# A chunked two-direction scan: one direction moved to the other quarters of the array, part of an element product given to GpSimd

## The chip, the cores and the metric

One core of a Trainium2 chip runs the whole kernel in one launch. The metric is the device time of that launch in microseconds, the median of several runs. The work of this case is all in one stage of the kernel, a recurrent scan of some 306 us out of about 2309 us.

## The reference, cut to what matters

The reference is a two-block model on 1024 tokens of width 1024, with 256 context tokens ahead. The change touches only the linear recurrence of the first block, run for 8 heads of 64 channels in both directions over 256 + 1024 tokens:

```
def wkv_scan(state0, r, decay, kk, b, v, k, reverse):
    def step(S, inp):
        r_t, w_t, kk_t, b_t, v_t, k_t = inp
        sa = jnp.einsum("bhvk,bhk->bhv", S, kk_t)
        S = (S * w_t[:, :, None, :] - sa[..., None] * b_t[:, :, None, :]
             + v_t[..., None] * k_t[:, :, None, :])
        return S, jnp.einsum("bhvk,bhk->bhv", S, r_t)
    ...
    S, ys = lax.scan(step, state0, xs, reverse=reverse)
```

All of it is float32.

## The kernel before, in words

**Stages.** `projections` (names `b_`) makes r, k, v, the decays and the keys, and stores four operands per direction and head pair to HBM (`ops`). `scan` (names `c_`) runs the recurrence; `mix_up` and the rest follow it and need its output `y`. The stages come one after the other.

**The scan.** The tokens are cut into chunks of 64; 4 context chunks and 16 sequence chunks make 20 steps (`STEPS`), `s` from 0. Direction `x` = 0 takes the chunks forwards, `x` = 1 backwards; both do step `s` at the same time. The 8 heads are 4 pairs `q`, and in a pair head `h` lies on partitions 0 to 63 or 64 to 127 (`ROWS[h]`). TensorE works with tiles of its array: a 64x64 matmul reads one half of the partitions and writes one half, so it occupies one of four quarters of the array. In what follows a quarter is named by the half it reads and the half it writes. Each float32 matmul appears in the trace as two records.

**TensorE's order in a step** is written out by hand (L1303 to L1325); every part is called for direction 0 and then for direction 1 by `both_dirs`:
- L1252 `chain_g_values`: both directions read the upper half and write lower and upper;
- L1214 `token_major`: 128x128 transposes of the next step's operands; L1261 `chain_g_state`: both directions read and write the same half (lower to lower, upper to upper);
- L1221 `triangles`: 64x128 matmuls of the next step; L1270 `chain_z`: both directions read both halves and write the lower one;
- L1277 `chain_s`, L1190 `blocks` (four of the twenty steps), L1232 `level_y` (32x32 tiles, next step), L1285 and L1288 `chain_y` (from step 4 on), L1242 `last_u` (next step).

A part's last matmul of a direction raises that direction's semaphore. ScalarE copies the results out of PSUM in the same order (`c_bk`, `c_gg`, `c_vz`, `c_raw`, `c_yd`, `c_ud`). VectorE masks the triangles (L1419, `c_lm`, two instructions per direction), makes the new state (L1423, L1425), and adds `y` in the later steps (L1406).

**The inverses.** Every four chunks (a batch `T`, five in all) need the inverse of triangular blocks. VectorE makes them in four parts (`blocks(T, part)`), one part behind each step's state; two batches go ahead of the loop in part (all of batch 0, parts 0 and 1 of batch 1), and step 0 has parts 2 and 3 of batch 1. Steps 1 to 12 have the parts 0 to 3 of batches 2, 3 and 4, one each. A product is a `dot`: an element product into `c_mul` (L1441, 512 to 2048 elements a partition) and a sum over the inner axis (L1442). The next step's L1419 stands behind the part on VectorE's queue. GpSimd only turns the finished inverse (L1527, `c_ti`) and, after the last one, splits weights for the next stage (L1530 to L1537).

**The DMA queue.** All DMAs here are issued in order by SyncE (SP): the stores of `ops` in `projections` (L220), 16 small stores of raw blocks (L312), a last operand store and a store of `mixd` (L238), then waits for all of them; the scan starts with the load of the first blocks (L1105, `c_nb`).

## Time and profile before

| | us |
|---|---|
| median of 3 runs | 2309.03 (2307.44 to 2312.41) |
| the profiled execution's own time | 2308.51 |
| its span | 2306.7 |
| scan, from its first load at 487.78 to its last VectorE instruction at 793.85 | 306.1 |

The span is the profiled part of that execution; the 1.8 us around it belong to the launch. PE is TensorE's matmuls, PEld its weight loads, DVE VectorE, ACT ScalarE, POOL GpSimd, SPq the DMAs that SyncE issues. A row of the timeline gives start, duration, engine, line, operation, output and inputs, shapes and how many instructions are merged; in square brackets stands the idle time ahead and what ended it.

### The profile page before, as it was taken

The numbers are of one execution on the slowest core, as the hardware profiler recorded it, in microseconds if no ns is written. First come the engines' busy times: TensorE is split into PE (matmuls) and PEld (weight loads), VectorE is DVE, ScalarE is ACT, GpSimd is POOL, SyncE is SP. The second block draws the span as 40 slices with busy tenths as digits, with TensorE's granted clock in tenths as the row PEclk, the third lists the DMA queues.
The fourth block names the chain that finished last, engine by engine and source line by source line (L and its number), as shares of the span: only waits on it lengthen the run. The fifth ranks groups of instructions, "written<-read, shape, count | busy, mean of one in ns | idle before, by whom it ended". The sixth has DMA issues, their size and how long they took to land. (4 is left out here: it accounts for less than half of the span.)

```text
span 2306.7 us, 36893 instructions
## 1 busy us (share of the span) xinstructions
PE 2108.3 (91%) x15096; PEld 1633.8 (71%) x15096; DVE 1543.7 (67%) x1999; ACT 872.2 (38%) x1411; POOL 782.9 (34%) x461
## 2 busy tenths in 40 slices
PE   7779999946999999899999989999899999999898
PEld 1656776745888777688887767887677777776666
DVE  5887767778887356888888892246636665545644
ACT  3434444412443355533333332354524343333320
POOL 0424344400003042777777753434222101111111
PEclk9889999976999999999999999999999999999999
DMA  7463343476765432122122255433212111102512
GB/s 285 176 214 112 108 141 112 133 210 177 201 198 140 134 119 86 52 83 79 70 80 83 83 187 205 152 114 109 84 56 83 56 32 61 65 19 68 197 55 82
DMA packets 180838, 271.07 MB, mean 118 GB/s; under 512 B 73784, under 2 KB 121528, under 8 KB 176320
## 3 DMA queue, kind: packets, MB, share of 16 engines
q1 hardware_dynamic: 176064, 251.94, 33.3%
q10 hardware_dynamic: 4608, 16.78, 2.0%
q8 instruction: 121, 1.98, 0.4%
q14 instruction: 45, 0.37, 0.1%
HBM read 200.48 MB, written 68.19 MB: 116 GB/s over the span
## 5 line engine op out<-in xcount | busy, mean ns | idle before, releaser
L105 PE MATMUL b_ps<-h_hi,b_wpool 128*128 128x512 f32 (+1 forms) x976 | 300.2, 385 | 20.3 <-issue 7.5
L2932 PE MATMUL g_ps<-g_h_hi,w 128*128 128x512 f32 x784 | 258.2, 401 | 5.0 <-ACT g_q L3125 5.0
L3245 POOL TENSOR_TENSOR w<-raw_down,w 128x1024 fp32r<-128x1024 f32 x38 | 94.3, 2482 | 460.0 <-ACT w L3103 460.0
L105 PEld LDWEIGHTS b_ps<-h_hi,b_wpool 128*128 128x128 f32 x976 | 182.4, 192 | 69.4 <-issue 19.8
L2201 DVE SCALAR_TENSOR_TENSOR e_vars<-grid,vec,e_vars 128x1024 f32<-128x1024 f32 x168 | 216.0, 1286 | 7.5 <-ACT e_vars L1948 4.2
L105 PE MATMUL b_ps<-h_lo,b_wpool 128*128 128x512 f32 (+1 forms) x488 | 184.5, 378 | 0.0
L2932 PEld LDWEIGHTS g_ps<-g_h_hi,w 128*128 128x128 f32 x784 | 147.6, 188 | 39.2 <-ACT g_q L3125 5.7
L2932 PE MATMUL g_ps<-g_h_lo,w 128*128 128x512 f32 x392 | 154.6, 394 | 0.0
L2613 POOL TENSOR_TENSOR g_down_lo<-raw_down,g_down_hi 128x1408 fp32r<-128x1408 f32 x26 | 86.6, 3335 | 141.6 <-ACT g_down_hi L2513 141.6
L2452 PE MATMUL g_pb<-g_z_hi,g_down_hi 128*128 128x512 f32 x286 | 114.6, 401 | 14.8 <-DVE g_down_lo L2690 9.8
L713 POOL TENSOR_TENSOR b_wpool<-raw_in,b_wpool 128x1024 fp32r<-128x1024 f32 x26 | 66.7, 2564 | 169.2 <-ACT b_wpool L511 169.2
L2452 PE MATMUL g_pb<-g_z_hi,g_down_lo 128*128 128x512 f32 x286 | 112.9, 395 | 0.0
L2452 PE MATMUL g_pb<-g_z_lo,g_down_hi 128*128 128x512 f32 x286 | 112.3, 393 | 0.0
L1928 ACT ACTIVATE e_main_hi<-e_raw_up 128x512 fp32r<-128x512 f32 x68 | 41.9, 622 | 172.1 <-DMA e_raw_up<-w_ffn 169.8
L105 PEld LDWEIGHTS b_ps<-h_lo,b_wpool 128*128 128x128 f32 x488 | 94.0, 193 | 16.8 <-issue 1.5
L2042 POOL TENSOR_TENSOR e_main_lo<-e_raw_up,e_main_hi 128x512 fp32r<-128x512 f32 x68 | 92.5, 1364 | 15.6 <-ACT e_main_hi L1928 15.6
L1527 POOL COPY c_ti<-c_ui 128x1024 f32<-128x1024 f32 x5 | 9.8, 1968 | 245.3 <-DVEq L1490 245.3
L3393 DVE COPY g_pt<-g_pb 128x512 f32<-128x512 f32 (+2 forms) x144 | 74.2, 552 | 18.9 <-PE g_pb L2991 17.6
L3025 PE MATMUL g_ps<-g_h_hi,w 128*128 128x512 f32 x224 | 77.9, 418 | 9.0 <-DVE g_sq L3401 3.3
L2932 PEld LDWEIGHTS g_ps<-g_h_lo,w 128*128 128x128 f32 x392 | 73.9, 189 | 16.2 <-issue 0.7
L3423 DVE SCALAR_TENSOR_TENSOR raw_down<-g_ps,g_gs 128x128 f32<-128x128 f32 x32 | 9.3, 292 | 108.1 <-PE g_ps L3007 108.1
L2250 DVE TENSOR_TENSOR e_z<-e_act_g,combine 128x512 f32<-128x512 f32 x42 | 63.6, 1553 | 22.4 <-ACT e_act_g L1961 22.3
(508 smaller groups left out, 5437.6 us busy)
## 6 DMA issues: line engine op xcount, KB each, us to landing
e_raw_up<-w_ffn SPq DMA_DIRECT2D x22, 1024.0 KB, 4.9
raw_down<-w_down SPq DMA_DIRECT2D x32, 704.0 KB, 4.1
c_op<-ops SPq DMA_DIRECT2D x40, 512.0 KB, 4.9
raw_down<-w SPq DMA_DIRECT2D x38, 512.0 KB, 3.7
b_xin<-ada_rows ACTq DMA_DIRECT2D x32, 512.0 KB, 5.1
ops<-b_xin SPq DMA_DIRECT2D x16, 1024.0 KB, 4.2
raw_in<-w SPq DMA_DIRECT2D x26, 512.0 KB, 4.2
zs<-e_z SPq DMA_DIRECT2D x21, 512.0 KB, 2.6
```

Source lines behind the costliest of these rows:

```text
L105: last = nc.tensor.matmul(out, w[:, k, :], x[:, k, cols], start=(k == 0 and n == 0), stop=(k == nk - 1 and n == 2))
L713: TT(weights(s)[1], raw, weights(s)[0].bitcast(F32), ALU.subtract).then_inc(sem("lo"), 1)
L1928: A(w_hi[slot], a_of[slot] if i < PLAIN else source[slot], ACT.Copy).then_inc(sem(f"w_hi{slot}"), 1)
L2042: TT(w_lo[slot], a_of[slot] if i < PLAIN else source[slot], w_hi[slot].bitcast(F32), ALU.subtract).then_inc(sem(f"w_lo{slot}"), 1)
L2201: STT(out=acc, in0=view, scalar=wt, in1=acc, op0=ALU.mult, op1=ALU.add).then_inc(sem("conv"), 1)
L2250: a = TT(z[:, cols(g)], act_g[:, cols(g)], val_of(g, i), ALU.mult)
L2452: mm = nc.tensor.matmul(bank_of(g, j), w[s][:, k], y[:, f], start=(f == 0 and i == 0), stop=(f == NFF - 1 and i == 2))
L2613: nc.gpsimd.tensor_tensor(w_lo[w_slot(n)], raw[:, n % 2], w_hi[w_slot(n)].bitcast(F32), ALU.subtract).then_inc(sem(f"w_lo{n % 2}"), 1)
L2932: mm = nc.tensor.matmul(out_bank, ww[w % 2][:, k], xx[g][:, k], start=(k == 0 and a == 0), stop=(k == KD - 1 and a == 2))
L3025: mm = nc.tensor.matmul(ps[1][:], ww[w % 2][:, k], xx[g][:, k], start=(a == 0 and b == 0), stop=(a == 1 + LAST and b == 2))
L3245: nc.gpsimd.tensor_tensor(w_lo[w % 2], raw[:, w % 2], w_hi[w % 2].bitcast(F32), ALU.subtract).then_inc(sem("lo"), 1)
L3393: nc.vector.tensor_copy(pt[:, h, at // P:to // P].rearrange("p b c -> p (b c)"), turned[u % 2][:, 0:to - at]).then_inc(sem("unturned"), 1)
```

## The change

The backward direction's operands are stored with the heads' halves exchanged and in another order (stores and loads L220, L1089, a table of decays exchanged by way of HBM), so that its `chain_g_values`, `chain_g_state`, `chain_z` and the first half of `chain_y` use the two quarters of the array that the forward direction doesn't use. These parts (and `blocks`) are no longer called once per direction: the matmuls of the two directions alternate, both directions' waits stand ahead of the part, and both semaphores are raised at its end. In the loop `triangles` of direction 0 now stands ahead of `chain_z` and that of direction 1 behind it.

In the two `dot`s with 2048 elements of each inverse batch (`c_nb,c_ui` in part 2, `c_ui,c_wi` in part 3) VectorE multiplies the first 10 of 16 rows (or 5 of 8), 1280 elements; GpSimd multiplies the other 768 into the same buffer. VectorE raises `part_due` ahead of its own product, and waits for `part_made` ahead of the sum.

```diff
-                sp.dma_start(d["ops"][x, :, s0:s0 + n // C, m],
-                             ops[:, j % 2, 0:n // C].rearrange("p s a c -> p s (a c)")).then_inc(sem(f"ops_stored{j % 2}"), 16)
+                for to, rows in (((slice(0, P), slice(0, P)),) if x == 0 else ((slice(0, HEAD), slice(HEAD, P)), (slice(HEAD, P), slice(0, HEAD)))):
+                    sp.dma_start(d["ops"][x, to, s0:s0 + n // C, m],
+                                 ops[rows, j % 2, 0:n // C].rearrange("p s a c -> p s (a c)")).then_inc(sem(f"ops_stored{j % 2}"), 16)
...
+            sp.dma_start(d["pends"], t["pend"][:, 1, NCTX:SLOTS]).then_inc(sem("pend"), 16)
...
+                            rows, of = slice(HEAD * h, HEAD * (h + 1)), slice(HEAD * (h ^ x), HEAD * ((h ^ x) + 1))
...
-    R, KK, B, K = range(4)
+    R, KK = (0, 3), (1, 2)
+    W_R, W_KK = (0, 1), (1, 0)
+    PAIR_RK, PAIR_BK = (slice(0, 2), slice(2, 4)), (slice(2 * C, 4 * C), slice(0, 2 * C))
...
-        OF_B, OF_K = ROWS
+        OF_B, OF_K = ROWS, ROWS[::-1]
+        state = lambda x, h: ROWS[h ^ x]
+        level = lambda x: slice(OF_B[x].start + HB * x, OF_B[x].start + HB * (x + 1))
...
+            for h in HEADS:
+                sp.dma_start(t["pend"][ROWS[h], 1, NCTX:SLOTS], d["pends"][ROWS[1 - h]]).then_inc(sem("pend"), 16)
...
-            def chain_g_state(x, s):
-                wait("p_gv", x, s + 1)
-                wait("sc", x, s + 1)
-                for q in range(PAIRS):
-                    for rows in ROWS:
-                        mm = nc.tensor.matmul(half(bank[x][2])[rows, q], op[x][s % 3][rows, KK, q], sc[x][s % 2][rows, q],
-                                              start=False, stop=(q == PAIRS - 1))
-                mm.then_inc(S("p_g", x), 1)
...
+            def chain_g_state(s):
+                for x in DIRS:
+                    wait("p_gv", x, s + 1)
+                    wait("sc", x, s + 1)
                 for q in range(PAIRS):
                     for h, rows in enumerate(ROWS):
-                        mm = nc.tensor.matmul(z_out(x, h)[OF_B, q], ud[x][s // BATCH % 2][rows, place(x, s), q], gg[x][rows, q], start=True, stop=True)
-                mm.then_inc(S("p_z", x), 1)
+                        mm = [nc.tensor.matmul(half(bank[x][2])[rows, q], op[x][s % 3][state(x, h), KK[x], q], sc[x][s % 2][state(x, h), q],
+                                               start=False, stop=(q == PAIRS - 1)) for x in DIRS]
+                for x in DIRS:
+                    mm[x].then_inc(S("p_g", x), 1)
...
+            def chain_z(s):
+                for x in DIRS:
+                    wait("u", x, s + 1)
+                    wait("gg", x, s + 1)
+                for q in range(PAIRS):
+                    for h, rows in enumerate(ROWS):
+                        mm = [nc.tensor.matmul(z_out(x, h)[OF_B[x], q], ud[x][s // BATCH % 2][rows, place(x, s), q], gg[x][rows, q],
+                                               start=True, stop=True) for x in DIRS]
+                for x in DIRS:
+                    mm[x].then_inc(S("p_z", x), 1)
...
+                        mm = nc.tensor.matmul(half(bank[x][2])[state(x, h), q], bk[x][s % 2][:, q, h ^ x], vz[x][s % 3][:, h, q], start=True, stop=True)
...
+            def chain_y(s):
+                for x in DIRS:
+                    wait("s1", x, s + 1)
+                out = [half(bank[x][2], 1) for x in DIRS]
                 for q in range(PAIRS):
                     for h, rows in enumerate(ROWS):
-                        mm = nc.tensor.matmul(out[rows, q], vz[x][s % 3][:, h, q], lm[x][s % 2][:, h, q, 0], start=False, stop=(q == PAIRS - 1))
-                mm.then_inc(S("p_y", x), 1)
+                        for x in DIRS:
+                            nc.tensor.matmul(out[x][rows, q], sc[x][s % 2][state(x, h), q], op[x][s % 3][state(x, h), R[x], q],
+                                             start=(q == 0), stop=False)
+                for x in DIRS:
+                    for q in range(PAIRS):
+                        for h, rows in enumerate(ROWS):
+                            mm = nc.tensor.matmul(out[x][rows, q], vz[x][s % 3][:, h, q], lm[x][s % 2][:, h, q, W_R[x]], start=False, stop=(q == PAIRS - 1))
+                    mm.then_inc(S("p_y", x), 1)
...
-                both_dirs(chain_g_values, s)
+                chain_g_values(s)
                 if more:
                     both_dirs(token_major, u)
-                both_dirs(chain_g_state, s)
+                chain_g_state(s)
                 if more:
-                    both_dirs(triangles, u)
-                both_dirs(chain_z, s)
+                    triangles(0, u)
+                chain_z(s)
+                if more:
+                    triangles(1, u)
                 both_dirs(chain_s, s)
                 if s in pres:
-                    both_dirs(blocks, pres[s])
+                    blocks(pres[s])
                 if more:
                     both_dirs(level_y, u)
                 if has_y(s):
-                    both_dirs(chain_y, s)
+                    chain_y(s)
...
+                if s == 0 and x == 1:
+                    dve.wait_ge(sem("pend"), 32)
...
+            def shared_dot(out, left, right, negate, nth):
+
+                rows, js, cols = *left.shape[1:], right.shape[2]
+                mine = slice(0, rows * 5 // 8)
+                prod = mul[:, 0:rows * cols * js].rearrange("p (i k j) -> p i k j", i=rows, k=cols)
+                dve.sem_inc(sem("part_due"), 1)
+                done(TT(prod[:, mine], bc(left[:, mine], 2, cols), bc(right.rearrange("p j k -> p k j"), 1, rows * 5 // 8), ALU.mult))
+                dve.wait_ge(sem("part_made"), nth)
...
-                    dot(w[:, :, low], n12, u22[:, :, low], False)
+                    shared_dot(w[:, :, low], n12, u22[:, :, low], False, 2 * T + 1)
...
-                    dot(u12[:, top], u11[:, top], w, True)
+                    shared_dot(u12[:, top], u11[:, top], w, True, 2 * T + 2)
...
+            def part_dot(left, right, nth):
+                rows, js, cols = *left.shape[1:], right.shape[2]
+                mine = slice(rows * 5 // 8, rows)
+                prod = mul[:, 0:rows * cols * js].rearrange("p (i k j) -> p i k j", i=rows, k=cols)
+                pool.wait_ge(sem("part_due"), nth)
+                nc.gpsimd.tensor_tensor(prod[:, mine], bc(left[:, mine], 2, cols), bc(right.rearrange("p j k -> p k j"), 1, rows - rows * 5 // 8),
+                                        ALU.mult).then_inc(sem("part_made"), 1)
...
+                part_dot(n12, u22[:, :, m // 2:m], 2 * T + 1)
+                part_dot(u11[:, 0:m // 2], w, 2 * T + 2)
```

TensorE's order for one step without `blocks` and `chain_y`, first as before (from L1252, `chain_g_values`, to L1242, `last_u`):

```order
L1252 MATMUL c_ps<-c_vz,c_lm 64x64 x16
L1214 MATMUL c_ps<-con,c_op 128x128 x8
L1261 MATMUL c_ps<-c_sc,c_op 64x64 x16
L1221 MATMUL c_ps<-c_op 128x128 x16
L1270 MATMUL c_ps<-c_gg,c_ud 64x64 x16
L1277 MATMUL c_ps<-c_vz,c_bk 64x64 x16
L1232 MATMUL c_ps<-c_td,c_lm 32x32 x16
L1242 MATMUL c_ps<-c_ud,c_yd 32x32 x16
```

And the same step with the change (L1266 is now `chain_g_values`, L1234 `triangles`, L1288 `chain_z`, L1297 `chain_s`):

```order
L1266 MATMUL c_ps<-c_vz,c_lm 64x64 x16
L1227 MATMUL c_ps<-con,c_op 128x128 x8
L1277 MATMUL c_ps<-c_sc,c_op 64x64 x16
L1234 MATMUL c_ps<-c_op 128x128 x8
L1288 MATMUL c_ps<-c_gg,c_ud 64x64 x16
L1234 MATMUL c_ps<-c_op 128x128 x8
L1297 MATMUL c_ps<-c_vz,c_bk 64x64 x16
L1245 MATMUL c_ps<-c_td,c_lm 32x32 x16
L1255 MATMUL c_ps<-c_ud,c_yd 32x32 x16
```

The number of matmuls is the same; the sixteen `triangles` now stand in two groups of eight on either side of `chain_z`.

GpSimd's order in the scan, before (L1527 turns the five inverses, the casts and subtractions are the next stage's weights):

```order
L1527 COPY c_ti<-c_ui 128x1024 x5
L1530 CAST c_hc<-c_hc 128x1024
L1532 TENSOR_TENSOR c_hc<-c_hc 128x1024
L1530 CAST c_hc<-c_hc 128x1024
L1532 TENSOR_TENSOR c_hc<-c_hc 128x1024
```

And with the change (L1560 is the part of the element product, L1569 the turn):

```order
L1560 TENSOR_TENSOR c_mul<-c_nb,c_ui 128x768
L1560 TENSOR_TENSOR c_mul<-c_ui,c_wi 128x768
L1569 COPY c_ti<-c_ui 128x1024
L1560 TENSOR_TENSOR c_mul<-c_nb,c_ui 128x768
L1560 TENSOR_TENSOR c_mul<-c_ui,c_wi 128x768
L1569 COPY c_ti<-c_ui 128x1024
```

Two products of 768 elements stand ahead of each of the five turns, ten in all.

## Rows read from the trace of the kernel before

**Rows 1.** Windows: length, busy of PE, PEld, DVE, ACT, POOL (count), PEclk, DMA share, GB/s.
```profile
487.78:523.80 36.02, 16.73 (x296) 15.39 (x296) 33.71 (x43) 5.32 (x10) 0.02 (x1) 0.64 0.84 234
...
564.57:722.00 157.43, 143.93 (x3582) 130.37 (x3584) 134.86 (x203) 64.72 (x189) 5.89 (x4) 0.92 0.65 181
...
745.23:779.01 33.78, 32.95 (x892) 30.00 (x890) 15.56 (x30) 13.58 (x42) 1.88 (x2) 1.00 0.36 105
```

**Rows 2.** VectorE's waits, 564.57 to 722.00 (total us, times, longest).
```profile
DVE c_lm L1419 <- PE c_ps L1221: 13.6, 6, 5.2
DVE c_s L1423 <- PE c_ps L1277: 2.7, 6, 0.8
DVE c_y L1406 <- PE c_ps L1288: 2.4, 2, 1.3
```

**Rows 3.** Timeline of TensorE, one late step.
```profile
774.63 1.15 PE L1252 MATMUL c_ps<-c_vz,c_lm 64*64 64x64 f32 x32
...
776.73 1.15 PE L1261 MATMUL c_ps<-c_sc,c_op 64*64 64x64 f32 x32
777.80 2.06 PE L1221 MATMUL c_ps<-c_op 64*128 64x128 f32 x32
...
781.22 1.23 PE L1277 MATMUL c_ps<-c_vz,c_bk 128*64 128x64 f32 x32 [0.28 <-ACT c_vz L1332]
782.37 0.60 PE L1232 MATMUL c_ps<-c_td,c_lm 32*32 32x32 f32 x32
782.90 0.68 PE L1285 MATMUL c_ps<-c_op,c_sc 64*64 64x64 f32 x16
```

**Rows 4.** Timeline of TensorE in the last step, where two parts meet.
```profile
786.82 0.27 PE L1261 MATMUL c_ps<-c_sc,c_op 64*64 64x64 f32 x1
786.87 0.22 PE L1252 MATMUL c_ps<-c_vz,c_lm 64*64 64x64 f32 x2
```

**Rows 5.** Timeline of VectorE, part 2 of an inverse and what follows.
```profile
645.56 3.79 DVE L1441 TENSOR_TENSOR c_mul<-c_nb,c_ui 128x2048 f32<-128x2048 f32 x1
649.39 2.29 DVE L1442 TENSOR_REDUCE c_wi<-c_mul 128x128 f32<-128x2048 f32 x1
651.82 1.92 DVE L1441 TENSOR_TENSOR c_mul<-c_ui,c_wi 128x1024 f32<-128x1024 f32 x1
...
655.03 2.48 DVE L1419 TENSOR_TENSOR c_lm<-c_ps,con_mixer 128x512 f32<-128x512 f32 x4
657.43 0.41 DVE L1423 TENSOR_TENSOR c_s<-c_sc,c_ps 128x256 f32<-128x256 f32 x1
```

**Rows 6.** Timeline of VectorE and GpSimd where both multiply at once.
```profile
69.07 2.83 DVE L918 TENSOR_TENSOR h_lo<-b_xin,h_hi 128x2560 fp32r<-128x2560 f32 x1
69.11 6.08 POOL L733 TENSOR_TENSOR h_lo<-b_xin,h_hi 128x1536 fp32r<-128x1536 f32 x1 [3.63 <-DVE b_xin L911]
...
735.59 2.35 POOL L1532 TENSOR_TENSOR c_hc<-c_hc 128x1024 fp32r<-128x1024 f32 x1
736.03 2.19 DVE L1425 TENSOR_TENSOR c_sc<-c_s,pend 128x256 f32<-128x256 f32 x1
```

**Rows 7.** Timeline of GpSimd around 722.
```profile
721.98 2.00 POOL L1527 COPY c_ti<-c_ui 128x1024 f32<-128x1024 f32 x1 [54.91 <-DVEq L1490]
723.92 1.04 POOL L1530 CAST c_hc<-c_hc 128x1024 fp32r<-128x1024 f32 x1
```

**Rows 8.** Windows with TensorE's granted clock, columns as in Rows 1.
```profile
562.00:564.00 2.00, 0.00 (x0) 0.00 (x0) 1.97 (x2) 0.00 (x0) 0.00 (x0) 0.50 0.00 0
570.00:572.00 2.00, 2.00 (x21) 1.88 (x18) 1.86 (x11) 0.25 (x1) 0.00 (x0) 0.50 0.74 116
...
604.00:606.00 2.00, 0.68 (x26) 0.43 (x22) 2.00 (x5) 0.28 (x1) 0.00 (x0) 1.00 1.19 368
```

**Rows 9.** DMAs issued by SyncE between the two stages.
```profile
480.87 0.45 SPq L220 DMA_DIRECT2D ops<-b_xin  x1
...
487.78 0.33 SPq L1105 DMA_DIRECT2D c_nb<-pb  x1
```

More of the change, by code:

```diff
@@ L1058, in scan, with tiles @@
                 if (s + 10) % BATCH < 2 and (s + 10) // BATCH < NBATCH}
+        def tiles(buf, m, row, col):
+            n, size = HB // (2 * m), 2 * m * (HB + 1)
+            start = row * HB + col
+            part = buf[:, 0:n * size].rearrange("p (b z) -> p b z", z=size)
+            end = start + m * HB
+            if end > size:
+                return buf[:, start:end].rearrange("p (b i c) -> p b i c", b=1, c=HB)[:, :, :, 0:m]
+            return part[:, :, start:end].rearrange("p b (i c) -> p b i c", c=HB)[:, :, :, 0:m]
         block = st.enter_context(nc.Block())
@@ L1184, in _ @@
         def _(pe):
-            def heads(out, *pairs):
-                for q in range(PAIRS):
-                    for n, (still, moving) in enumerate(pairs):
-                        for rows in ROWS:
-                            last = nc.tensor.matmul(out[rows, q], still[rows, q], moving[rows, q],
-                                                    start=(n == 0), stop=(n == len(pairs) - 1))
-                return last
             def wait(name, x, value):
@@ L1244, in last_u, with chain_g_values @@
                 mm.then_inc(S("p_u", x), 1)
-            def chain_g_values(x, s):
-                wait("lm", x, 2 * s + 2)
-                wait("s1", x, s)
-                wait("yo", x, s - NCTX)
+            def chain_g_values(s):
+                for x in DIRS:
+                    wait("lm", x, 2 * s + 2)
+                    wait("s1", x, s)
+                    wait("yo", x, s - NCTX)
                 for q in range(PAIRS):
                     for h, rows in enumerate(ROWS):
-                        mm = nc.tensor.matmul(half(bank[x][2])[rows, q], lm[x][s % 2][OF_K, h, q, 1], vz[x][s % 3][OF_K, h, q],
-                                              start=(q == 0), stop=False)
-                mm.then_inc(S("p_gv", x), 1)
@@ L1256, in chain_g_state @@
-            def chain_g_state(x, s):
-                wait("p_gv", x, s + 1)
-                wait("sc", x, s + 1)
-                for q in range(PAIRS):
-                    for rows in ROWS:
-                        mm = nc.tensor.matmul(half(bank[x][2])[rows, q], op[x][s % 3][rows, KK, q], sc[x][s % 2][rows, q],
-                                              start=False, stop=(q == PAIRS - 1))
-                mm.then_inc(S("p_g", x), 1)
-            def chain_z(x, s):
-                wait("u", x, s + 1)
-                wait("gg", x, s + 1)
+                        mm = [nc.tensor.matmul(half(bank[x][2])[rows, q], lm[x][s % 2][OF_K[x], h, q, W_KK[x]], vz[x][s % 3][OF_K[x], h, q],
+                                               start=(q == 0), stop=False) for x in DIRS]
@@ L3556, in constants @@
     before = [s < u, s > u]
-    parts["tri"] = np.concatenate([tri(m) for b in before for m in (b | (s == u), b)], 1)
+    parts["tri"] = np.concatenate([tri(m) for x, b in enumerate(before) for m in ((b | (s == u), b), (b, b | (s == u)))[x]], 1)
     first = np.tile(np.arange(C), BANK // C)[None, :]
```

83 lines of the change are left out of this document (39 added, 44 removed).

## The prediction, made before the changed kernel ran

> **What bounds the kernel now.** I read the timeline of the scan first, then windows of it, then VectorE's waits, and last the places where GpSimd works beside VectorE. The scan falls into three stretches, and each has another bound. Ahead of step 0 VectorE makes the first inverse: in the 36.02 us up to its first mask it is busy 33.71, TensorE 16.73 [rows 1]. In the twelve inverse steps (from the mask at 564.57 to that at 722.00, 157.43 us) the two are close: TensorE busy 143.93, VectorE 134.86 [rows 1]. VectorE waits there 13.6 + 2.7 + 2.4 = 18.7 us for TensorE [rows 2], so without any wait it would need 157.4 - 18.7 = 138.7 us. That is the floor which VectorE's queue sets, since the next step's mask stands behind the inverse's part. In the late steps, which have no inverse, TensorE is busy 32.95 of 33.78 us for three steps, 11.26 us each [rows 1]: there it alone sets the end.
>
> **TensorE's quarters.** A part of 32 records in two quarters takes 1.15 us, and the next may start 1.07 us after it (776.73 to 777.80) [rows 3]. Does a third or fourth quarter run beside them? The last step shows it: a record of L1261 (lower half to lower half, direction 0) starts at 786.82 while L1252 (upper half to both halves, direction 1) is still putting in two records at once at 786.87 [rows 4]. So a quarter takes its records when it is free, whatever the others do. The 32x32 part issues 32 records in 0.53 us (782.37 to 782.90) [rows 3], so issue isn't a limit before about 17 ns a record, and I take 0.54 for a part of four quarters. Each of `chain_g_values`, `chain_g_state` and `chain_z` gets shorter by 0.53 us; of `chain_y` the two first halves, 0.61 each (the 0.68 of L1285 less its 0.07 of overlap) [rows 3], become one of 0.55, so 0.67. The wait of 0.28 us for ScalarE ahead of `chain_s` [rows 3] goes too, because direction 1's triangles (half of 2.06) stand there now. Sum for a late step: 3 x 0.53 + 0.67 + 0.28 = 2.54 us, from 11.26 to 8.72.
>
> What is late next: direction 1's triangles come behind `chain_z`, and VectorE masks them (half of 2.48) before it makes any state; then come state, scaling and state, about 0.42 each with gaps of 0.03 to 0.04 [rows 5], and `chain_y` now waits for the states of both directions. That is 0.2 (end of the matmuls) + 1.24 + 1.35 = 2.8 us behind the triangles, of which `chain_s` (1.15) and `level_y` (0.53) cover 1.7. So 1.1 us of wait come back, and 0.1 ahead of `chain_z`, whose two copies on ScalarE are now covered by half the triangles. The step becomes 8.72 + 1.2 = 9.9 us, a gain of 1.3.
>
> The Trainium skill's page "TensorEngine Tiling (Array Packing)", section "Restrictions and Gotchas", says that different row tiles can't use the same PSUM bank at once. By that rule L1261, whose two halves write one bank, would be slower than L1252, whose two tiles are in one row; both take 1.15 us, so the trace doesn't bear it out. Were it so with four quarters, the parts would keep their length, and the time would be that of the third rival below.
>
> **GpSimd's share.** The change supposes that GpSimd multiplies beside VectorE. The rows say that it can't. At 69.07 VectorE begins a product of two SBUF tensors, at 69.11 GpSimd one; VectorE takes its 2.83 us, and GpSimd, with 1536 elements, 6.08: 2.83 of waiting and 3.25 of work [rows 6]. At 736.03 it is the other way round: L1425 takes 2.19 us, because GpSimd's subtraction lasts until 737.94 [rows 6]. The inverse's product L1441 has two inputs in SBUF as well. VectorE raises `part_due` and goes on at once, so it begins first; GpSimd then multiplies its 768 elements while VectorE waits for `part_made`. The two run one behind the other.
>
> What GpSimd needs for 768 elements isn't in the trace. At 3.25 us for 1536 it would be 1.6; but one operand is read with a step, and a copy of 1024 elements that reads with a step takes 2.00 against 1.04 for a plain cast [rows 7], 0.94 ns an element more: 0.7 us more with one such operand at the 2.35 us per 1024 of L1532 (1.8), or 1.9 times the 1.8. So 1.6 to 3.4; I take 1.8 + 0.7 = 2.5, since L1532 and L1527 are the nearest rows. VectorE saves 3/8 of 3.79 = 1.42, and pays 0.1 for raising a semaphore (the gap of 0.14 at 651.68, where one is raised already, against 0.04) [rows 5]. Each of the ten products so costs 2.5 + 0.1 - 1.4 = 1.2 us on VectorE, between 0.3 and 2.1.
>
> The page "GPSIMD Engine Reference", section "Instruction dispatch", of the Trainium skill gives a floor of 2.5 cycles per element for two inputs, at 1.2 GHz. An estimate by that page is 1.6 us for 768, and the total below would be some 9 us less; no run here shows a product with this step on GpSimd.
>
> **The sum, stretch by stretch.** Ahead of the scan SyncE issues one more half store and the decays' store behind the store that takes 0.45 us at 480.87; the first load of the scan waits for all of them [rows 9]: +0.9. The twelve other split stores lie beside TensorE's dense work in the stage before and cost nothing; if a weight load queued behind them were late, 0.4 each. The decays' two loads stand ahead of loads that are not needed until step 4: nothing. The first inverse is all VectorE's: two products, +2.4. Step 0 holds two more, again with TensorE idle behind them: +2.4; ahead of them TensorE's shorter parts bring VectorE's next mask forward by about 1.0, since the mask of direction 1 now waits for `chain_z`: -1.0.
>
> In the twelve inverse steps the shorter parts put TensorE mostly behind VectorE, so the floor counts: 138.7 + 6 x 1.2 = 145.9. It isn't reached. In a part-2 step VectorE needs 655.03 - 645.56 = 9.5 us for the part [rows 5] and 4.0 for masks and states, 13.5 us from mask to mask, 14.7 with the share, and TensorE some 9, so it idles for 5 us. After such idleness the granted clock is 0.50, the lower level of 1.2 GHz, as at 562 to 564, and stays there while TensorE works again (570 to 572: busy all the time, 0.50); at 604 to 606, after less idleness, it is 1.00 [rows 8]. One such drop in each of the three batches makes TensorE late by 1.5 to 2 us, and the parts with `blocks`, where ScalarE's two copies now come one behind the other, by some more: +6. So 152, a gain of 5.4. Late steps: three at 1.3, -3.9; the two ahead of them, where GpSimd's subtractions hold up L1425 as before, 0.9 each, -1.8; the tail, which is a chain of latencies, -0.8.
>
> Total: 0.9 + 2.4 + 2.4 - 1.0 - 5.4 - 3.9 - 1.8 - 0.8 = -7.2. From the profiled execution's 2308.5 (0.5 under the median, which is less than the runs differ by) this gives **2301**. With GpSimd at its bounds (0.3 and 2.1 for each of ten products) it is 2292 and 2310.
>
> **Rivals.**
> *The products do run side by side.* Then GpSimd ends about 2.6 us after the start, and a product costs 1.0 less than before instead of 1.2 more. For: another access pattern on VectorE, which takes 1.85 ns an element, may leave the port free. Against: both places in [rows 6]. The first inverse and step 0 gain 2 x 2.0 instead of losing 4.8; the inverse steps have a floor of 138.7 - 6 = 132.7, and with TensorE's remaining 6 end near 138.7, -18.7. Total 0.9 - 2.0 - 3.0 - 18.7 - 6.5 = -29.3: 2279.
> *TensorE's clock falls in every inverse step (slower).* TensorE's shorter parts leave it idle in all of them, not in three. For: a drop shows at 562. Against: 604 to 606. At 1.2 GHz the way from a mask to the next (waits of 1.3, `level_y`, `chain_y`, `last_u`, `chain_g_values`, transposes, `chain_g_state`, half the triangles: about 6 us at full clock without the 1.3) doubles to 12, and with the mask's 2.48 a step takes 14.4: 12 x 14.4 = 172.8, +15.4. Total 3.3 + 1.4 + 15.4 - 6.5 = +13.6: 2322. It decides once more than half of the twelve steps run at the low clock.
> *The other quarters bring nothing (slower).* The parts keep their length, so only the new waits stay: late steps 0.4 longer, +2; the waits of [rows 2] remain and six products add about 6; ahead +5.7. Total +13.7: 2322. Against it: [rows 4].
>
> **Chances and range.** The forecast 0.55, side by side 0.15, clock 0.18, quarters 0.12. The likeliest case alone spans 2292 to 2311. The range that takes in the first rival's time and most of the slower ones, which reach down towards 2312 where they hold in part, is 2279 to 2320. No change is within 0.2% (4.6 us) of 2309, about what a measurement can tell. Of the forecast's 0.55 some 0.36 lie under 2304, 0.16 between, 0.03 above 2314; with the rivals: faster 0.51, the same 0.19, slower 0.30.
>
> **What would show it.** `chain_g_state` and its like at about 0.75 us long instead of 1.15; late masks 9.9 us apart; L1560 on GpSimd at over 4 us when its wait behind VectorE is counted, and 2.5 from the end of VectorE's product; VectorE idle by 2.5 ahead of each of ten sums; the granted clock low once per batch. I am wrong if GpSimd's product ends with VectorE's, if the four-quarter parts still take over 1.0 us, or if the low clock fills the inverse steps.

## The result, and the profile after

The changed kernel takes 2315.48 us (median of 20 runs, 2304.69 to 2326.76), the kernel before beside it 2306.02 (20 runs, 2301.05 to 2323.1). The ratio is 1.0033, 95% interval 1.0020 to 1.0046: slower by 7.6 us, 4.6 to 10.6. (The two medians stand 9.5 apart, inside that interval; what follows goes by the ratio.) The forecast was 2301 and faster. The profiled execution took 2320.37 us (span 2318.6), 11.9 us of span more than that of before. It is 4.9 us above its kernel's median, so a pair of single traces has more to explain than the timed runs do.

Four places say most of it. First the windows of the changed kernel, columns as in [rows 1] and answering to them:

```profile
491.81:529.41 37.60, 11.50 (x296) 10.09 (x296) 35.07 (x43) 5.54 (x10) 4.37 (x3) 0.59 0.82 225
570.20:722.82 152.62, 126.41 (x3584) 110.92 (x3584) 138.40 (x203) 66.01 (x192) 19.97 (x10) 0.88 0.67 187
746.65:783.30 36.65, 29.88 (x893) 26.30 (x897) 15.13 (x30) 13.89 (x42) 1.93 (x2) 0.95 0.36 107
```

The twelve inverse steps are shorter (152.62 for 157.43 in this pair of traces), and TensorE is busy 126.41 us there for 143.93. But three late steps take 36.65 us where they took 33.78, although TensorE is busy 3.1 us less. That is the surprise: it has less to do and is done later.

TensorE's timeline in the late steps (start, length, line, tiles, count, idle time and what ended it), which answers to [rows 3]:

```profile
739.50 1.04 PE L1307 MATMUL c_ps<-c_op,c_sc 64*64 64x64 f32 x32 [2.32 <-DVE c_s L1451]
740.48 1.97 PE L1312 MATMUL c_ps<-c_lm,c_vz 128*64 128x64 f32 x32
...
756.36 0.69 PE L1277 MATMUL c_ps<-c_sc,c_op 64*64 64x64 f32 x32
756.98 1.16 PE L1234 MATMUL c_ps<-c_op 64*128 64x128 f32 x16
758.07 0.69 PE L1288 MATMUL c_ps<-c_gg,c_ud 64*64 64x64 f32 x32
758.70 0.60 PE L1234 MATMUL c_ps<-c_op 64*128 64x128 f32 x5
761.47 0.94 PE L1234 MATMUL c_ps<-c_op 64*128 64x128 f32 x11 [2.17 <-issue]
```

The four-quarter parts are what they were forecast to be: `chain_g_state` (L1277) is 0.69 us long and the next part starts 0.62 after it, against 1.15 and 1.07 [rows 3]. Two things stand between them now. One is a wait for VectorE of 2.32 us ahead of `chain_y`, followed by a second half at half the speed (1.97 us for the 1.15 that the same part has elsewhere). The other is an idle time of 2.17 us in the middle of a part, after five of its sixteen records, which ends on "issue": no semaphore was waited for.

The same wait from the other engines' side, and the first of the shared products (VectorE and GpSimd in one timeline):

```profile
512.46 2.21 POOL L1560 TENSOR_TENSOR c_mul<-c_nb,c_ui 128x768 f32<-128x768 f32 x1 [42.09 <-DVEq L1467]
512.47 4.44 DVE L1468 TENSOR_TENSOR c_mul<-c_nb,c_ui 128x1280 f32<-128x1280 f32 x1
...
736.40 2.34 POOL L1574 TENSOR_TENSOR c_hc<-c_hc 128x1024 fp32r<-128x1024 f32 x1
...
737.05 1.98 DVE L1453 TENSOR_TENSOR c_sc<-c_s,pend 128x256 f32<-128x256 f32 x1
```

The product runs one behind the other, as forecast, but GpSimd is first: 2.21 us for its share, and VectorE's 4.44 us are these and some 2.2 of its own. At 737.05 VectorE's scaling (0.42 us when alone) stands behind GpSimd's subtraction until 738.74, as at 736.03 in [rows 6]. That hold made TensorE wait in the kernel before too, but only 0.78 us; its step took 12.59 us there, the three behind it 11.26:

```profile
738.61 0.68 PE L1285 MATMUL c_ps<-c_op,c_sc 64*64 64x64 f32 x16 [0.78 <-DVE c_s L1423]
```

The groups of products, of before (first fence) and after: line, tiles, count, busy us, mean ns.

```profile
L1441 DVE TENSOR_TENSOR c_mul<-c_nb,c_ui 128x2048 f32<-128x2048 f32 x5 | 18.9, 3787 | 0.0
L1441 DVE TENSOR_TENSOR c_mul<-c_ui,c_wi 128x2048 f32<-128x2048 f32 x5 | 18.3, 3652 | 0.1
```

```profile
L1468 DVE TENSOR_TENSOR c_mul<-c_nb,c_ui 128x1280 f32<-128x1280 f32 x5 | 22.3, 4456 | 0.1
L1468 DVE TENSOR_TENSOR c_mul<-c_ui,c_wi 128x1280 f32<-128x1280 f32 x5 | 21.4, 4273 | 0.3
L1560 POOL TENSOR_TENSOR c_mul<-c_nb,c_ui 128x768 f32<-128x768 f32 x5 | 11.8, 2368 | 145.1 <-DVEq L1467 145.1
```

Ten products hold VectorE for 43.7 us instead of 37.2, 0.65 more each.

SyncE's issues between the two stages (start, length of issue), answering to [rows 9]:

```profile
463.37 9.81 SPq L221 DMA_DIRECT2D ops<-b_xin  x3
473.23 9.14 SPq L313 DMA_DIRECT2D pb<-h_spare  x16
482.41 1.26 SPq L221 DMA_DIRECT2D ops<-b_xin  x2
483.72 1.94 SPq L316 DMA_DIRECT2D pends<-pend  x1
485.70 2.18 SPq L239 DMA_DIRECT2D mixd<-c_row  x1
491.81 0.32 SPq L1121 DMA_DIRECT2D c_nb<-pb  x1
```

The last operand store's two halves take 1.3 us to issue where the whole took 0.45, the decays' store 1.9, and the issue of `mixd` grew from 0.58 to 2.18. From 463.37 to the scan's first load it is 28.44 us; before, 25.92. The long issues are not the sixteen small stores' doing, for the 0.45 and 0.58 of before stood behind the same sixteen. What stands ahead of them is an operand store. Behind the whole one at 471.31 two issues were long in the kernel before as well, the second and the third of the sixteen:

```profile
472.34 1.24 SPq L312 DMA_DIRECT2D pb<-h_spare  x1
473.63 0.75 SPq L312 DMA_DIRECT2D pb<-h_spare  x1
...
481.37 0.58 SPq L238 DMA_DIRECT2D mixd<-c_row  x1
```

In the changed kernel the decays' store and `mixd` stand in that place behind two halves, and take more.

Last, windows over the late steps, the tail and the next stage's start, of before (first fence) and after, columns as in [rows 1]; the clock is the third figure from the end:

```profile
722.00:779.01 57.01, 53.95 (x1446) 48.69 (x1442) 28.54 (x50) 22.64 (x70) 21.44 (x15) 1.00 0.51 142
779.01:793.90 14.89, 13.73 (x400) 12.29 (x396) 7.37 (x16) 4.65 (x16) 0.00 (x0) 1.00 0.01 3
793.90:804.00 10.10, 8.78 (x31) 5.95 (x32) 3.11 (x3) 2.12 (x2) 0.00 (x0) 1.00 0.78 286
```

```profile
722.82:783.30 60.48, 49.72 (x1438) 43.89 (x1442) 28.15 (x50) 21.90 (x66) 21.49 (x15) 0.92 0.48 133
783.30:800.00 16.70, 12.72 (x400) 11.30 (x400) 7.46 (x16) 4.88 (x16) 0.00 (x0) 0.83 0.01 3
800.00:810.00 10.00, 8.75 (x24) 5.24 (x25) 1.88 (x2) 1.06 (x1) 0.00 (x0) 0.77 0.78 287
```

Before, TensorE worked at 2.4 GHz from 722 to 804 without a break; now it falls to 1.2 GHz for part of each of these stretches.

**What the idle times on "issue" are.** Twelve times in the scan TensorE stands still with its semaphores reached. I counted TensorE's records (matmuls, weight loads, waits) up to the one that ends each, and looked for the last 16 KB instruction fetch (DMA queue 8) before it. Worked out from the trace's records, not a view:

```
from    idle  line   record    of 256  fetch began  resumed after it
552.90  0.83  L1255   5058      194     551.30       +2.43
558.07  0.28  L1288   5314      194     555.91       +2.44
636.89  2.64  L1255   8642      194     637.19       +2.34
651.88  1.13  L1255   9409      193     650.26       +2.74
657.32  0.36  L1288   9666      194     655.23       +2.46
677.70  0.66  L1266  10690      194     675.91       +2.46
700.17  1.32  L1307  11713      193     698.77       +2.72
721.54  1.11  L1234  12738      194     720.14       +2.51
749.57  0.46  L1245  14017      193     747.55       +2.48
753.23  1.48  L1266  14274      194     752.39       +2.32
759.30  2.17  L1234  14530      194     758.97       +2.50
775.47  0.75  L1307  15297      193     773.82       +2.40
```

All twelve (the first expectation below counts eleven) end at the same place modulo 256 records, 193 or 194, and 2.3 to 2.75 us after a 16 KB fetch began: TensorE had come to the end of a block of 256 instructions, and the next was still on its way. They sum to 13.2 us, against 4.3 in five such places before, and 5.9 in a second trace of the kernel before. These idle times are called stalls below.

The Trainium skill's page "Runtime: NRT & Kernel Launch", section "Instruction fetch mechanics", says that instructions are refilled in blocks of 256 (16 KiB) while the block ahead runs, and that crossing a block is mostly hidden. The trace agrees on the block's size; hidden it isn't in these twelve places.

### The profile page after: what moved, and what is told of

It reads as the page before. It is cut to its first block and busy times, and to the rows that moved or that the text cites. A ratio compares the mean times of both kernels' runs of the same rounds, so it can differ in the third digit from the quotient of the medians.

```text
span 2318.6 us, 36973 instructions
## 1 busy us (share of the span) xinstructions
PE 2083.9 (90%) x15096; PEld 1603.4 (69%) x15096; DVE 1547.4 (67%) x1999; ACT 872.7 (38%) x1411; POOL 804.7 (35%) x471
## 5 line engine op out<-in xcount | busy, mean ns | idle before, releaser
L3197 ACT ACTIVATE g_s<-g_logits,g_mx 128x128 f32<-128x128 f32 (+7 forms) x64 | 49.6, 775 | 69.2 <-DVE g_mx L3416 67.9
```

What stands on the lines that cost most here:

```text
L3197: A(s2[:, h, 0:keys(p)], logits[:, h, 0:keys(p)], ACT.Exp, bias=mx[:, h:h + 1], accum_out=den[:, i % 2, h:h + 1]).then_inc(sem(f"weights{h ...
```

## Experiments

Times are medians; ratios are to runs of the kernel before on the same chip, with 95% intervals; 0.001 is 2.3 us.

**The parts of the change, one at a time.** The quarters (with their stores) without the shared products:

```
-  shared_dot(w[:, :, low], n12, u22[:, :, low], False, 2 * T + 1)
+  dot(w[:, :, low], n12, u22[:, :, low], False)
...
-  part_dot(n12, u22[:, :, m // 2:m], 2 * T + 1)
```

> The changed kernel with VectorE making its whole products again (no share for GpSimd): the four quarters, the split stores and the decays' exchange alone. Theory: TensorE runs into the end of its instructions. In the changed kernel's trace it stands still 11 times in the scan with no wait on any semaphore, 13.2 us together against 4.3 in five places before, always just at every 256th instruction and always about 2.4 us after a 16 KB instruction fetch began; a block of 256 instructions that runs faster than its successor is fetched gains nothing. By that theory these stalls stay at 8 us or more here, late steps stay at 11 to 12.5 us, and the kernel wins back only what the ten products cost, about 0.75 us each: 2306 to 2310. Rival: the share for GpSimd is what lost the time and the stalls come from it (through the masks and states that come late): then stalls fall to about 4 us, late steps to 10 us, and the time to 2299 or less.

2308.34 us, ratio 1.0013 (1.0003 to 1.0024). Stalls 15.5 us; the five late steps, from VectorE's first mask for step 14 (u14) to that for step 19 (u19), 60.2 us. The theory's side: the stalls belong to the quarters, not to GpSimd's share.

The shared products in the kernel before:

```
+  shared_dot(w[:, :, low], n12, u22[:, :, low], False, 2 * T + 1)
...
+  part_dot(n12, u22[:, :, m // 2:m], 2 * T + 1)
```

> The kernel before with GpSimd's three eighths of the products alone (no other quarters, no new stores). Each product stage took 2.21 + 2.23 = 4.44 us in the changed kernel's trace against 3.7 to 3.8 before, so +0.7 each and 0.1 for the semaphores. Four of the ten lie where VectorE alone sets the end (+3.2), six in the inverse steps, where TensorE bounds about as often (0 to +4.8): 2309 to 2314, with TensorE's unexplained stalls at 3 to 6 us as before. Rival: the products carry the whole loss, 2315 or more. Second rival: hidden in the inverse steps and not slower at all, 2306.

2312.11 us, ratio 1.0030 (1.0020 to 1.0041): +6.9 us (4.6 to 9.5), with 4.1 us of stalls. Ten products by 0.65 us of VectorE are 6.5, so hardly anything of them is hidden. Single traces don't tell where: its first inverse is 1.6 us longer, the rest is within what two traces differ by.

The stores in the kernel before (direction 1 in halves, the decays stored and loaded back):

```
-  sp.dma_start(d["ops"][x, :, s0:s0 + n // C, m], ops[:, j % 2, ...])
+  for rows in ((slice(0, P),) if x == 0 else (slice(HEAD, P), slice(0, HEAD))):
+      sp.dma_start(d["ops"][x, rows, s0:s0 + n // C, m], ops[rows, j % 2, ...])
...
+  sp.dma_start(d["pends"], t["pend"][:, 1, NCTX:SLOTS])
```

> The kernel before with the stores of the change alone: direction 1's operands stored in two halves (to the same place as before), the decays stored behind the last of them and loaded again in the scan. Theory: at the end of the stage SyncE's issues take 1.26, 1.94 and 2.18 us where one took 0.45 and one 0.58, so the scan's first load comes about 2.5 us later: 2308.5. Rival, as it was predicted: +0.9, so 2307. A third: the stage's end moves with something else from run to run, and there is no difference.

2310.77 us, ratio 1.0022 (1.0009 to 1.0036). From SyncE's last operand stores to the scan's first load 28.47 us, the 28.44 of the changed kernel to 0.03: the 2.5 us are shown. Whether the rest of its 5 us (2 to 8) is real isn't settled; the interval holds 2.5. One late step of its trace takes 14.75 us: a scaling is held for 2.47 us by a subtraction, TensorE waits 1.49, and the granted clock falls to 0.50 behind it. So the old scan's late steps aren't safe from the hold either; they take 59.9 us here.

Together: products 6.9, quarters with stores 3.0, sum 9.9 for the whole's 7.6 (4.6 to 10.6). Less 2.5 for the stores, the quarters, on which all of the forecast's gain rested, give about nothing.

**Is it late instructions?** Direction 1's load half a step later:

```
   for x in DIRS:
       if s + 2 < STEPS:
+          if x:
+              wait("p_z", x, s + 1)
           load(x, s + 2)
```

> As the kernel with the quarters alone, but SyncE issues direction 1's operand load only once chain_z of the step is done, half a step behind direction 0's, in place of right behind it. Theory: an instruction fetch starts late because it stands behind data on its DMA engine (it starts 0 to 4.3 us after the block before it has begun); with the loads apart the backlog is about half, fetches start at most some 2.5 us late, stalls fall by half or more, and the kernel is 3 to 5 us faster than the one with the quarters alone. Rival: fetches are late by TensorE's own doing and not by data, so the stalls stay and nothing is gained; or direction 1's operands come too late for its transposes, and it is slower.

Stalls fall from 15.5 to 4.7 us as the theory has it, the late steps from 60.2 to 57.1; yet the time is 2308.64 (1.0017, 1.0004 to 1.0030). TensorE now waits 3.1 us for a late load in an early step, and the low clock remains. The expected 3 to 5 us didn't come. So the stalls depend on when the operands are loaded, and the whole loss doesn't go with them.

Seven eighths of the operand loads left out, in the changed kernel and in the one before:

```
-  sp.dma_start(op_ring[x][u % 3][:], d["ops"][x, :, slot])
+  if u < 3:
+      sp.wait_ge(sem("zeroed"), 2 * u + x + 1)
+  sp.dma_start(op_ring[x][u % 3][:, 0:1], d["ops"][x, :, slot, 0:1])
```

> The changed kernel with seven eighths of the scan's operand loads left out: each step loads one pair of eight, the rest of the six buffers is zeroed by GpSimd while the first inverse is made (so the outputs aren't the reference's). TensorE's instructions are the same. Theory: instruction fetches come late because they stand behind operand data. Then they start within 1.5 us of the block before them, the scan's 13.2 us of stalls at block ends fall below 4 us, and late steps without a stall are 10.1 us apart, the same as where no stall fell in the kernel with the loads half a step apart (10.14). Rival: the fetches are late by TensorE's own sequence, and the stalls stay above 8 us with hardly any operand traffic.

> The kernel before with the same seven eighths of the operand loads left out and the buffers zeroed in the same way. It is the control for the changed kernel without these loads: 4.3 us of stalls should fall to 1 or less, late steps stay at 11.26 us, so it gains at most 4 us, where the changed kernel should gain 8 or more. If both gain the same, the loads cost something other than late fetches.

Stalls 2.3 and 1.2 us. Between 540 and 790 us the fetch of a block began over 2 us after the block before it had begun in 6 of 47 cases without the loads (I expected all within 1.5 us), and in 22 of 45 in the changed kernel (counted from the traces' records). So fetches come late beside operand data. That isn't new with the change, for in two traces of the kernel before it is 14 of 45 and 18 of 46. And both kernels gained: 2306.76 (0.9998, 0.9983 to 1.0012) and 2298.53 (0.9973, 0.9955 to 0.9990). The changed kernel gains 8 us, as expected; the one before gains 6, where I expected 4 at most. Without the loads the change still costs 0.0025, of 0.0033. The first is known to some 0.002 only, the second to 0.001, so the timed runs don't tell how much of the loss the stalls explain. What stays of late steps in the changed kernel's trace without the loads (start, length, engine, line):

```profile
763.55 1.26 POOL L1584 TENSOR_TENSOR c_w_lo<-c_w_raw,c_w_hi 128x512 fp32r<-128x512 f32 x1
763.64 1.45 DVE L1455 TENSOR_TENSOR c_sc<-c_s,pend 128x256 f32<-128x256 f32 x1
...
765.57 0.69 PE L1309 MATMUL c_ps<-c_op,c_sc 64*64 64x64 f32 x32 [1.79 <-DVE c_s L1453]
...
768.21 1.13 PE L1268 MATMUL c_ps<-c_vz,c_lm 64*64 64x64 f32 x32
```

GpSimd's subtraction is 0.1 us ahead of VectorE's scaling, which takes 1.45 for 0.42; `chain_y` waits 1.79 for 0.77; and the part at 768.21 takes 1.13 for 0.69, at the lower clock of 1.2 GHz. Five late steps take 56.6 us so.

**GpSimd's subtractions behind the scaling.** The same kernel, and GpSimd starts them only when VectorE has made its last scaling of a step:

```
   for k in range(KD // 2):
+      pool.wait_ge(S("sc", 1), 15 + k // 2)
...
   for n in range(3):
+      pool.wait_ge(S("sc", 1), (17, 17, 20)[n])
```

> The changed kernel with seven eighths of the operand loads left out (outputs not the reference's), and GpSimd's seven subtractions in the late steps started only behind VectorE's last scaling of a step, where VectorE has no operation with two SBUF inputs for some 9 us. Theory: with both the late fetches and GpSimd's holds gone the late steps get what was forecast for them: five steps from the mask of u14 to that of u19 in 5 x 10.14 = 50.7 us, 52 at most (56.6 with the loads left out alone, 57.0 in the kernel before), and the waits of 2.3 and 1.8 us ahead of chain_y become 0.77. Rival: the waits are VectorE's own latency, and the steps stay at 56 us.

2300.96 us (0.9996, 0.9979 to 1.0012). The five late steps take 10.88, 10.18, 10.15, 10.20 and 10.27 us, 51.7 in sum. TensorE's timeline of one:

```profile
745.33 1.16 PE L1236 MATMUL c_ps<-c_op 64*128 64x128 f32 x16
746.42 0.69 PE L1290 MATMUL c_ps<-c_gg,c_ud 64*64 64x64 f32 x32
747.05 1.22 PE L1236 MATMUL c_ps<-c_op 64*128 64x128 f32 x16
748.20 1.15 PE L1299 MATMUL c_ps<-c_vz,c_bk 128*64 128x64 f32 x32
749.28 0.81 PE L1247 MATMUL c_ps<-c_td,c_lm 32*32 32x32 f32 x32
750.87 0.69 PE L1309 MATMUL c_ps<-c_op,c_sc 64*64 64x64 f32 x32 [0.77 <-DVE c_s L1453]
```

This is the late step of the forecast, with its one wait ahead of `chain_y` (0.77, forecast 1.1). The 4.9 us that the trace gains over the kernel without the gate don't show in the timed runs (0.9996 for 0.9998); their intervals are too wide to deny them either. The same gate with the loads whole, in the kernel with the quarters alone:

> The quarters alone, with GpSimd's subtractions of the late steps gated in the same way, loads whole. Theory: the two holds go, and the low clock that follows them; the stalls at block ends stay (0 to 5 us in the late steps), so from u14 to u19 53 to 57 us where the quarters alone took 60.2, and 2303 to 2307 in all. Rival: the gain goes into the stalls, 60 us and 2308.

2303.10 us (0.9991, 0.9973 to 1.0008). The holds are gone in the trace, the waits for VectorE ahead of `chain_y` 0.77 or less, but 14.5 us of stalls fell in the scan, 4.4 of them in the late steps, and these took 58.5 (53 to 57 expected). The traced execution was the slowest of the twelve (2315.80), so its steps are hardly typical.

**Order and clock.** Both triangles ahead of `chain_z`:

```
-  triangles(0, u) ... chain_z(s) ... triangles(1, u)
+  both_dirs(triangles, u) ... chain_z(s)
```

> The quarters alone, with the triangles of both directions ahead of chain_z, as the order was before (the change puts chain_z between them). Theory: the wait of 0.77 us ahead of chain_y in each late step stands behind direction 1's masks; made 0.6 us earlier, it shrinks to about 0.2, and 0.3 comes back ahead of chain_s for the copies on ScalarE: 0.3 us for each of eight steps, 2 us at most and inside what the runs differ by: 2306 to 2309. Rival: VectorE's states and not the masks set chain_y's start, and nothing moves; 2308.

2310.18 us (1.0027, 1.0011 to 1.0044): not better. In each late step 0.67 to 0.75 us of waiting for ScalarE came back ahead of `chain_s`, more than the 0.3 expected, and 16.5 us of stalls fell in this trace.

Fillers where TensorE waits:

```
+  def fill(s, n, b=3):
+      for _ in range(n):
+          nc.tensor.matmul(bank[0][b][:], t["c_ident"], ...)   # 128x512
```

> The kernel with the quarters and the loads half a step apart, and in the last seven steps TensorE multiplies 128x512 zero-value tiles (results unused) where it waits: two ahead of level_y and four ahead of chain_y in the first of them, two and then one ahead of chain_y in the others, three more in the last step; about 0.5 us each at full clock, 16 in all. Theory: the late steps lose their gain to the low clock that follows these waits (17 us at the lower level between 720 and 800, none in the kernel before); with the waits filled the clock stays high, and the scan ends 4 us earlier or more, so 2304. Rival: the waits and the latency behind them set the steps, the clock doesn't: then the fillers change nothing or cost up to 2 us.

2308.01 us (1.0008, 0.9996 to 1.0020). The clock stays at 1.00 from 720 to 850, and next to nothing is lost between the last scaling and the end of the next stage's first four matmuls (0.2 us more than before, 3.2 without fillers). But a filler takes 1.06 us, not 0.5, so by my estimate they cost 2 to 3 us more than the waits they fill, and the late steps don't get shorter (56.9 for 57.1). The expectation fell by half: in the trace the clock mattered in the tail, and what it costs in the late steps isn't shown.

**All together, and what is left of it.**

```
+  nc.scalar.dma_start(d["ops"][1, to, ...], ops[rows, 1, ...])   # job 5's halves
+  nc.scalar.dma_start(d["pends"], t["pend"][:, 1, NCTX:SLOTS])
```

> What the runs point to, together: quarters without GpSimd's share; its subtractions gated; direction 1's operand load half a step behind direction 0's from step 2 on; one 128x256 filler of about 0.5 us on TensorE ahead of chain_y from step 13 on and three in the last step, so that the tail and the next stage's first matmuls run at full clock; and the last operand halves and the decays stored through ScalarE's queue, which is idle then, while SyncE is issuing. Theory: 2.5 us at the stage's end, 4 to 6 in the late steps, 1.5 to 3 behind the scan against the quarters alone (2308.3): 2298 to 2301, faster than both kernels. Rival: each gain is given back further on, and it is 2305 or more.

2304.32 us (0.9995, 0.9983 to 1.0008), above the 2298 to 2301 expected. The stage's end takes 26.7 us, so 1.75 of the 2.5 come back. Late steps 58.6 us: with the loads half a step apart the transposes waited 1.2 and 2.3 us for one of them. The next kernels therefore load as before.

> The kernel before once more, for a second trace of it: how far one trace differs from another where nothing is changed. If the twelve inverse steps, 157.4 us in the first trace, come out between 154 and 158 and the late steps at 57 again, differences of 3 us in the inverse steps between single traces tell nothing.

Twelve steps 155.0 us, late steps 57.3, stalls of 5.9 us, and 6.7 us less than the first trace behind the scan, with nothing changed. A single trace tells the inverse steps to 3 us and nothing of the later stages.

> The quarters with the gated subtractions and the loads as they were, and the last operand halves and the decays stored through ScalarE's queue. Theory: in the kernel that put everything together the stage's end took 26.7 us from SyncE's last operand stores to the scan's first load, against 28.45 with the change's stores and 25.92 before, so 1.75 us come back here, on top of the kernel with the gate alone (2303.1): 2301 to 2302. Rival: the gate's gain was luck and it stands at 2305 to 2307, the same as before.

2303.26 us (1.0000, 0.9987 to 1.0014), above the 2301 to 2302 expected. Its trace reaches the next stage 9.8 us before that of before, the best of all; the timed runs don't bear it out.

> As that one, with four fillers of 128x256 on TensorE in the last step, where it waits for ScalarE and VectorE. Theory: in the kernels with the quarters 2 to 3.4 us are lost between the last scaling and the next stage's first matmuls, which run at the low clock; with the fillers the clock stays high (none were lost in the two kernels that had them), so 1.5 to 3 us less than without them: 2299 to 2300, the fastest of all. Rival: the tail is a chain of copies and states, and the clock there costs nothing: no difference.

2301.44 us, ratio 0.9985 (0.9972 to 0.9999): the only kernel with the reference's outputs whose interval ends below the kernel before, by 3.5 us, and barely. Of seven kernels built to win something back one may do that by luck. SyncE's end of the stage in it:

```profile
472.28 12.65 SPq L313 DMA_DIRECT2D pb<-h_spare  x16
...
477.25 1.96 SPq L313 DMA_DIRECT2D pb<-h_spare  x1
479.25 2.18 SPq L313 DMA_DIRECT2D pb<-h_spare  x1
...
484.97 0.45 SPq L239 DMA_DIRECT2D mixd<-c_row  x1
489.13 0.34 SPq L1125 DMA_DIRECT2D c_nb<-pb  x1
```

And TensorE's tail in it, then in the changed kernel:

```profile
787.88 1.15 PE L1316 MATMUL c_ps<-c_lm,c_vz 128*64 128x64 f32 x32
790.88 1.96 PE L1743 MATMUL e_means<-c_y,con 128*128 128x512 f32 x4 [1.85 <-PEq L83]
```

```profile
797.41 1.97 PE L1312 MATMUL c_ps<-c_lm,c_vz 128*64 128x64 f32 x32
801.25 3.57 PE L1727 MATMUL e_means<-c_y,con 128*128 128x512 f32 x4 [1.86 <-PEq L83]
```

With the clock up, the last two parts take 0.8 and 1.6 us less. The sixteen `pb` stores (first row; the next two rows are two of them) issue in 12.65 us instead of 9.14. The two long issues of 1.96 and 2.18 us have only moved: ScalarE issues the halves at 475.80 and 476.51, and behind them it is `pb` stores on SyncE that take as long as the decays' store and `mixd` did. That is why not all 2.5 us come back.

## Why the prediction was wrong, step by step

The forecast was wrong in its direction. The traces' spans differ by 11.9 us. By the forecast's stretches, forecast and measured (trace of after less trace of before):

```
                               forecast  measured
stage ahead begins its end         0       +1.5   differs from trace to trace: 458.4 to 463.5
stores at the stage's end        +0.9      +2.5
first inverse                    +2.4      +1.6
steps 0 and 1                    +1.4       0.0
twelve inverse steps             -5.4      -4.8
five late steps                  -5.7      +3.5
tail, and four matmuls after it  -0.8      +3.4
stages behind them                 0       +4.1   not settled: 6.7 between two traces of before
```

- *Quarters side by side*: right. 0.69 us and 0.62 from start to start (forecast 0.54), and by [rows 4] already. The page "TensorEngine Tiling (Array Packing)" of the Trainium skill, section "Restrictions and Gotchas", would have kept 1.15, since both row tiles write one bank; the trace doesn't bear it out.
- *One product behind the other*: right, and GpSimd's 2.1 to 2.4 us for 768 elements are near the 2.5 taken. Wrong in who begins, and in size: 0.65 us each on VectorE, not 1.2. Timed alone, the ten cost 6.9 us, nearly all of these 6.5.
- *Twelve inverse steps, -5.4*: -4.8 in this pair of traces, but partly by luck, because two errors cancel. With products at 0.65 the forecast's floor is 142.6 and not 145.9; what came on top of it was 10 us and not 6. Against the three traces with the old scan and its own products (154.2, 155.0 and 157.4) the gain is 1.6 to 4.8.
- *Clock once per batch*: too seldom. In the twelve steps 36 us are at the lower level of 1.2 GHz, 24 and 19 in the two traces of the kernel before.
- *Late steps, -3.9 and -1.8*: **this step failed.** The first two took 0.6 us more than before, the last three 2.9. I worked out the next bound from waits on semaphores alone, and took TensorE's work and VectorE's latency for all that stays. The 9.9 us were nearly right (10.15 to 10.27 measured), but only with two other things taken away. One is the stalls at block ends. They are there in the kernel before (4.3 and 5.9 us), and with the shorter parts they come to 11 to 16 us in the six traces that load as the change does. The other is GpSimd's subtractions, which stood in [rows 6]: the forecast let each of them take 0.4 us of a step's gain (0.9 for 1.3), and one made TensorE wait 2.32 us, where a free step waits 0.77. The late steps took 60.5 us, 8.8 more than with stalls and holds taken away (51.7): 4.9 are stalls from 749 to 776, 1.6 the hold, and 2.4 is left. That stands in the two steps in which the granted clock falls to 0.50 (at 740 behind the wait of 2.32, at 777 behind waits of 0.77 and 0.75), 1.2 and 1.4 us, so I put it down to the clock; no run shows that price by itself. The clock doesn't fall behind every wait: it stayed at 1.00 behind the stalls of 1.48 and 2.17. That the three add up so in one execution is arithmetic, not an experiment.
- *Tail, -0.8*: failed. I called it a chain of latencies and so untouched by the clock. In the changed kernel TensorE waits 0.31, 0.84 and 0.74 us there, the granted clock is 0.50 from 794 to 804, and the next stage's first four matmuls take 3.57 us instead of 1.96. From the last scaling to their end seven traces with the quarters lose 1.6 to 3.2 us against the kernel before, one 0.2, and the three with fillers 0.2 or less (the expectations above say 2 to 3.4). One trace with the old scan, without the operand loads, loses 1.4 too.
- *Stores, +0.9*: mis-sized, 2.5. I counted issues of 0.45 us from [rows 9], of a DMA with no operand store close ahead of it; the two issues that follow the two halves took 1.9 and 2.2.

Of the rivals, "the quarters bring nothing" had the sign for a false reason: the parts do get shorter, and the gain is given back. The rival of the clock put its price in the inverse steps; it fell due in the late ones and the tail.

What stays open: what the quarters gain in the whole by themselves. The kernel with the quarters alone less 2.5 for its stores gives a loss of 0.5 us, anywhere from a gain of 1.8 to a loss of 3.0; the whole less the products and the stores gives a gain of 1.8. With the gate, the stores through ScalarE and the fillers in the tail the kernel is 3.5 us below the one before, 0.2 to 6.5. How the loss divides between stalls, holds and clock is read from traces alone; the timed runs are too close together to tell.

## What to carry to other kernels

When a part gets shorter, ask of every hold and every supply that its length covered: a lock between two other engines, the fetch of the next instructions, the clock. A busy share of 98% for TensorE hid all three here. Ten small costs on VectorE, which sets the pace or nearly does (6.9 us together), outweighed a gain on the engine beside it.

## What was not expected of the hardware

- TensorE's instructions arrive in 16 KB blocks by DMA; it resumes 2.3 to 2.75 us after a late fetch begins (12 cases after, 5 before). With operand loads 22 of 45 fetches began over 2 us after the block before; with an eighth of them 6 of 47. The count alone doesn't give the stalls: with the quarters alone it is 15 of 46 and 15.5 us, with the loads half a step apart 15 of 46 and 4.7 us.
- Shortly behind an operand store two DMA issues are long: 1.24 and 0.75 us behind a whole one, 1.9 and 2.2 behind two halves, 0.4 to 0.65 for most others at this stage's end. Where ScalarE issues the halves, its own next issue is long (1.94), and so are two on SyncE (1.96 and 2.18).
- VectorE raises `part_due` and then begins its own product, yet GpSimd, which waits for it, began first in all ten products, by 0.01 us in three (512.46 and 512.47) and 0.23 in seven, and VectorE waited all of its 2.1 to 2.4 us.
